# A Hymba block on one core: two quadrant sums of the gate weight made by accumulating transfers, and pair 2's spatial products placed later

## The reference, cut to what matters

```python
h = rms_norm(x, norm_mix_pre)                 # x: 2048 x 1024, float32
z = h @ w_in                                  # q, k, v, and the columns u and v of the gating unit
g_in = gelu(z[..., o3:])                      # 1024 columns: u (512), v (512)
vn = layer_norm(v, ln_g, ln_b)
s_out = u * (W_masked @ vn + b)               # 4 groups, blocks of 128 positions: the spatial products
```

## Time and profile before

| | us |
|---|---|
| median of 3 runs (1841.42 to 1842.73) | 1842.46 |
| the profiled execution | 1840.42 |
| its span, first to last instruction | 1838.6 |
| PE busy in it | 1818.6 (99%) |
| DVE busy | 1274.8 (69%) |
| ACT busy | 740.7 (40%) |
| POOL busy | 148.9 (8%) |

### The profile page before, as it was taken

One profiled execution on the slowest core, in us unless ns is written; L12 is line 12 of the kernel. 1 busy time (PEld: TensorE's weight loads), 2 busy tenths in 40 slices (PEclk: granted clock), 3 DMA queues, 4 the chain that ended last, 5 costly groups with the idle time before them and its releaser, 6 DMA issues.

```text
span 1838.6 us, 24806 instructions
## 1 busy us (share of the span) xinstructions
PE 1818.6 (99%) x9322; PEld 1527.1 (83%) x9322; DVE 1274.8 (69%) x1625; ACT 740.7 (40%) x1278; POOL 148.9 (8%) x162
## 2 busy tenths in 40 slices
PE   9999999999999999999999999999999999999998
PEld 7788899988888888888888888888887888888887
DVE  8879777864568777776767777676776755554564
ACT  7776566753345323233234322323223222332342
POOL 1111222210000000000000000000000000000244
PEclk9999999999999999999999999999999999999999
DMA  6886743345666333332344423432235664534655
GB/s 236 293 318 259 264 196 153 116 150 206 221 262 232 127 108 112 99 108 86 108 121 172 141 86 108 125 106 88 86 111 179 257 231 159 195 124 176 248 204 189
DMA packets 134324, 310.78 MB, mean 169 GB/s; under 512 B 6384, under 2 KB 85232, under 8 KB 121072
## 3 DMA queue, kind: packets, MB, share of 16 engines
q1 hardware_dynamic: 134256, 309.90, 48.1%
HBM read 207.64 MB, written 102.24 MB: 169 GB/s over the span
## 4 chain that ended last, share of the span: by engine, by line
PE 86%; DVE 2%; issue 0%; POOL 0%; ACT 0%; DVEq 0%; POOLq 0%
PE T L2028 7%; PE T L2029 7%; PE T L2030 7%; PE ZB L2365 4%; PE ZB L2367 4%; PE ZB L2366 4%; PE T L2367 4%; PE T L2365 4%; PE T L2366 4%; PE S L2367 3%; PE S L2365 3%; PE S L2366 3%; PE ZA L2367 3%; PE ZA L2365 3%; PE ZA L2366 3%; PE ZA L2028 2%
## 5 line engine op out<-in xcount | busy, mean ns | idle before, releaser
L2028 PE MATMUL T<-tb_hi,sb_hi 128*128 128x512 f32 x616 | 239.9, 390 | 1.3 <-DVE sb_lo L1914 1.2
L2030 PE MATMUL T<-tb_hi,sb_lo 128*128 128x512 f32 x616 | 239.7, 389 | 0.0
L2029 PE MATMUL T<-tb_lo,sb_hi 128*128 128x512 f32 x616 | 239.7, 389 | 0.0
L1201 ACT ACTIVATE sb_hi<-sb_raw 128x1408 fp32r<-128x1408 f32 x56 | 77.4, 1381 | 290.6 <-PE T L2030 275.8
L1777 DVE TENSOR_TENSOR t_lo<-t_raw,t_hi 128x1024 fp32r<-128x1024 f32 (+1 forms) x126 | 169.0, 1397 | 0.1
L2365 PE MATMUL ZB<-s_hi,t_hi 128*128 128x512 f32 x352 | 137.1, 389 | 1.1 <-DVE t_lo L1777 1.1
L2028 PEld LDWEIGHTS T<-tb_hi,sb_hi 128*128 128x128 f32 x616 | 115.6, 188 | 26.5 <-issue 1.9
L2365 PE MATMUL T<-s_hi,t_hi 128*128 128x512 f32 x352 | 137.0, 389 | 0.0
L2366 PE MATMUL ZB<-s_lo,t_hi 128*128 128x512 f32 x352 | 137.0, 389 | 0.0
L2366 PE MATMUL T<-s_lo,t_hi 128*128 128x512 f32 x352 | 136.9, 389 | 0.0
L2367 PE MATMUL ZB<-s_hi,t_lo 128*128 128x512 f32 x352 | 136.9, 389 | 0.0
(11 more groups left out here) (314 smaller groups left out, 4275.4 us busy)
## 6 DMA issues: line engine op xcount, KB each, us to landing
t_raw<-w_gu SPq DMA_DIRECT2D x42, 1024.0 KB, 4.7
act_d<-ac SPq DMA_DIRECT2D x22, 1792.0 KB, 8.0
sb_raw<-act_d SPq DMA_DIRECT2D x56, 704.0 KB, 4.1
h_d<-quarters SPq DMA_DIRECT2D x8, 1792.0 KB, 6.6
s_raw<-h_d SPq DMA_DIRECT2D x14, 1024.0 KB, 6.4
lb_hi<-hl_d SPq DMA_DIRECT2D x6, 1792.0 KB, 7.2
lb_lo<-hl_d SPq DMA_DIRECT2D x6, 1792.0 KB, 11.5
tb_raw<-w_dn SPq DMA_DIRECT2D x6, 1536.0 KB, 6.4
```

The lines of the kernel that those rows point to most:

```text
L1201: e.activation(sb_hi[it % 2][:, :, :], sb_raw[it % 2][:, :, :], ACT.Copy).then_inc(sb_hi_done, 1)
L2028: e.matmul(out_ap, lhi, rhi, start=start, stop=False)
L2029: e.matmul(out_ap, lhi, rlo, start=False, stop=False)
L2030: return e.matmul(out_ap, llo, rhi, start=False, stop=stop)
```

## The change

R3 and R4 are no longer subtracted on DVE. ACT writes a negated copy into the place of the sum (of B12 for R3, of R2 for R4), and a transfer issued by POOL then adds a quadrant from DRAM (B22, B21) onto it. POOL waits for all the constants before the first, and for the first to land before the second. The orders on ACT, DVE and PE are changed around it, and the numbers that waits on `w_sum` and `gel_done` count to are adjusted.

```diff
 # POOL, ahead of rstd_x(0)
+            def add_block(dst, src):
+                e.dma_start(dst[:, :, :], src, accum_op=ALU.add).then_inc(w_added, 16)
+            e.wait_ge(consts, 16 * 6)
+            e.wait_ge(b12_read, 2)
+            add_block(wu_raw[3], w_uv[B22, :, :, :])
+            e.wait_ge(w_sum, 3)
+            e.wait_ge(w_added, 16)
+            add_block(wu_raw[6], w_uv[B21, :, :, :])
             rstd_x(0)
-            e.wait_ge(consts, 16 * 6)
 # ACT
             wu_hi_part(6, wu_b12, slice(2, 4))
+            e.activation(wu_raw[3][:, :, :], wu_b12[:, :, :], ACT.Copy, scale=-1.0).then_inc(b12_read, 1)
...
+            e.wait_ge(in_done, 3)
+            e.activation(wu_raw[6][:, :, :], wu_raw[2][:, :, :], ACT.Copy, scale=-1.0).then_inc(w_sum, 1)
             stats_x(0)
-            e.wait_ge(w_sum, 3)
-            wu_hi_part(6, wu_raw[6])
             uv_copy(1, 0)
-            e.wait_ge(w_sum, 4)
+            e.wait_ge(w_added, 16)
             wu_hi_part(3, wu_raw[3])
             uv_copy(1, 1)
             gelu_v(0, 1)
             stats_x(1)
+            e.wait_ge(w_added, 32)
+            wu_hi_part(6, wu_raw[6])
+            scale_xq(2)
+            left_hi(2, 0)
             gelu_u(0, 0)
             gelu_v(0, 0)
             gelu_u(0, 1)
-            scale_xq(2)
-            left_hi(2, 0)
...
+            gelu_v(1, 0)
             gelu_u(1, 0)
-            gelu_v(1, 0)
             gelu_u(1, 1)
 # DVE: the two subtractions
-                if i == 3:
-                    e.tensor_tensor(wu_raw[3][:, :, :], wu_b22[:, :, :], wu_b12[:, :, :], ALU.subtract).then_inc(w_sum, 1)
-                if i == 6:
...
-                    e.tensor_tensor(wu_raw[6][:, :, :], wu_b21[:, :, :], wu_raw[2][:, :, :],
-                                    ALU.subtract).then_inc(w_sum, 1)
 # DVE: the order
-            wu_sum(6)
-            wu_sum(3)
+            e.wait_ge(w_sum, 3)
             wu_lo_part(2, wu_raw[2], 7)
             left_lo(1, 2)
-            wu_lo_part(3, wu_raw[3], 9)
+            wu_lo_part(3, wu_raw[3], 8)
             norm_stats(0, 1)
+            normed(0, 1)
             uv_u2(1)
-            wu_lo_part(6, wu_raw[6], 8)
+            wu_lo_part(6, wu_raw[6], 9)
             uv_u3(1)
-            normed(0, 1)
             left_sums(2)
...
             uv_upper(1)
             gate(0, 1)
-            gate(0, 0)
-            uv_lower(1)
             left_lo(2, 2)
             normed(1, 1)
+            uv_lower(1)
+            gate(0, 0)
             norm_stats(1, 0)
             normed(1, 0)
 # PE, behind product (j, i); spatial(j - 1, 1) comes first
-                    if i in (2, 4):
+                    if i in ((3, 4) if j == 2 else (2, 4)):
                         spatial(j - 1, 1 - i // 4)
```

More of the change, by code:

```diff
@@ L202, in build_kernel @@
     w_in_loaded, b11_rest = [sem(f"w_in_loaded{i}") for i in range(4)], sem("b11_rest")
-    b12_rest, b12_hi, b12_split = sem("b12_rest"), sem("b12_hi"), sem("b12_split")
+    b12_rest, b12_read, b12_split = sem("b12_rest"), sem("b12_read"), sem("b12_split")
     id_zero, pool_consts = sem("id_zero"), sem("pool_consts")
     xq_scaled, lsum_done, lhi_done, lsplit = sem("xq_scaled"), sem("lsum_done"), sem("lhi_done"), sem("lsplit")
-    w_sum, w_hi_done, w_split = sem("w_sum"), sem("w_hi_done"), sem("w_split")
+    w_sum, w_hi_done, w_split, w_added = sem("w_sum"), sem("w_hi_done"), sem("w_split"), sem("w_added")
     hl_out, norm_step = sem("hl_out"), sem("norm_step")
@@ L390, in load_wout @@
                 e.dma_start(wout_raw[c][:, :], w_out[chunk(c), :]).then_inc(wout_in[c], 16)
-            e.wait_ge(w_sum, 4 + 3)
+            e.wait_ge(w_sum, 3 + 3)
             e.dma_start(cs[:, :, :], rope).then_inc(cs_in, 16)
-            e.wait_ge(w_sum, 4 + 4)
+            e.wait_ge(w_sum, 3 + 4)
             e.wait_ge(w_split, 9 + 3)
@@ L793, in gelu_v @@
                     e.wait_ge(w_split, 2)
-                    e.wait_ge(w_sum, 4)
+                    e.wait_ge(w_sum, 2)
                     e.activation(dst[:, :], GU[0][1 + par], ACT.Gelu, scale=r).then_inc(gel_done, 1)
@@ L819, in wq_hi_part @@
                     src = {R1: wq_r1, R2: wq_r2}[t] if t in (R1, R2) else wq_raw[i]
-                    e.wait_ge(w_sum, 4 + {R1: 1, R2: 2, R3: 3, R4: 4}[t])
+                    e.wait_ge(w_sum, 3 + {R1: 1, R2: 2, R3: 3, R4: 4}[t])
                 e.activation(wq_hi[i][:, :, :], src[:, :, :], ACT.Copy).then_inc(w_hi_done, 1)
@@ L831, in _ @@
             e.wait_ge(w_in_loaded[B12], 16)
-            e.activation(wu_hi[6][:, 0:2, :], wu_b12[:, 0:2, :], ACT.Copy).then_inc(b12_hi, 1)
+            e.activation(wu_hi[6][:, 0:2, :], wu_b12[:, 0:2, :], ACT.Copy).then_inc(b12_read, 1)
             e.wait_ge(b12_rest, 16)
             wu_hi_part(6, wu_b12, slice(2, 4))
+            e.activation(wu_raw[3][:, :, :], wu_b12[:, :, :], ACT.Copy, scale=-1.0).then_inc(b12_read, 1)
             e.wait_ge(w_in_loaded[B22], 16)
@@ L1312, in gate @@
                 e.wait_ge(g_full, n + 1)
-                e.wait_ge(gel_done, 4 * j + (2, 4)[par])
+                e.wait_ge(gel_done, 4 * j + (3 if j == 1 else 2, 4)[par])
                 if j:
@@ L1323, in norm_stats @@
                 src = (bv12, bv22)[par]
-                e.wait_ge(gel_done, 4 * j + (3, 1)[par])
+                e.wait_ge(gel_done, 4 * j + (2 if j == 1 else 3, 1)[par])
                 e.bn_stats(st6[:, par, :], src[:, :]).then_inc(norm_step, 1)
@@ L1385, in wq_sum @@
                     e.wait_ge(w_split, 9 + 1)
-                    e.wait_ge(w_sum, 4 + 1)
+                    e.wait_ge(w_sum, 3 + 1)
                     e.tensor_tensor(wq_r2[:, :, :], wq_in[B22][:, :, :], wq_r1[:, :, :],
@@ L1395, in wq_sum @@
                     e.wait_ge(w_in_loaded[B21], 32)
-                    e.wait_ge(w_sum, 4 + 2)
+                    e.wait_ge(w_sum, 3 + 2)
                     e.tensor_tensor(wq_raw[6][:, :, :], wq_in[B21][:, :, :], wq_r2[:, :, :],
@@ L1410, in _ @@
             first_lo(1)
-            e.wait_ge(b12_hi, 1)
+            e.wait_ge(b12_read, 1)
             e.tensor_tensor(wu_lo[6][:, 0:2, :], wu_b12[:, 0:2, :], wu_hi[6][:, 0:2, :].bitcast(F32),
@@ L2082, in uv_product @@
                     if i == 0:
-                        e.wait_ge(gel_done, 4 * (j - 2) + 2)
+                        e.wait_ge(gel_done, 4 * (j - 2) + (3 if j == 3 else 2))
                     if i == 1 and j == 2:
```

3 lines of the change are left out of this document (removed).

## The result

The changed kernel took 1845.9 us (median of 20 runs, 1843.12 to 1847.88); the kernel before, in as many runs beside it, 1841.01 (1839.81 to 1842.73). The ratio is 1.0024, with a 95% interval from 1.0017 to 1.0031: slower by 4.9 us, where the forecast had 1.95. The median of before that the prediction started from (1842.46, 3 runs) was 1.45 high against the larger number of runs, so the absolute forecast of 1844.4 stands nearer to 1845.9 than its sum deserves. What follows goes by the differences. The profiled execution took 1845.38, 4.96 more than that of before.

A forecast was written before the change was run, and what follows sets the result against it. PE was taken as the bound (busy 99%), capping any gain at 3.5 us of waits; +1.35 at product (2, 0) and +0.6 at spatial (2, 1) took 1842.46 to 1844.4 us, range 1840.5 to 1848.5.

The forecast's parts named there:

- First negated copy free, `bp1`'s wait of 0.6 gone: ACT's first negated copy fills idle time at no cost; product (1, 4) loses its 0.6 us wait for `bp1`.
- R3 hidden: First adding transfer lands at about 33, R3 is wanted by about 38 for product (1, 3), so no wait.
- The adds, 6.5 and 8 us: POOL's two accumulating 1 MB transfers take 6.5 and 8 us, bounds 4.8 and 11.8 each.
- s = 42.2: Pair 1's second squares on ACT start at 42.2, bounds 40.6 and 43.8, after later-issued `xs` transfers; before, 41.12.
- The chain behind s: From pair 1's second squares through POOL and DVE: product (1, 6) at s+7.6, `left_sums(2)` at s+7.4.
- The limit for the second add: ACT's `wu_hi6` and `scale_xq(2)` stay slack if the second add lands by s+2.3 = 44.5.
- Product (2, 0) at 54.1: On PE, product (2, 0) starts at 54.1, 1.35 us later than 52.74, bounds -0.25 and +2.9.
- Pair 2: The removed 2.0 us norm wait at spatial (1, 1) is swallowed at spatial (2, 1), and 0.6 us is lost.
- The sum: Product (2, 0) +1.35 and spatial (2, 1) up to +0.6 give +1.95 us; bounds 1842.3 to 1846.8.
- Slow adds: Rival, 0.18: ACT's `wu_hi6` waits for a second add past 44.5; at 11.8 us each, 1849.8 us.
- POOL held by DVE: Rival, 0.07: the adds' descriptors are written only when DVE pauses, first at about 36; 1847.6 us.
- Gain: Rival, 0.20: `xs` lands in 5.2 us and the gated tiles' store does not bind; about -1.6, 1840.9 us.

The follow-up runs named there:

- no addition: Changed kernel with POOL's two transfers as plain loads of the same 1 MB, the sums left out: 1841.38 us, ratio 1.0005 to the kernel before.
- add early: Changed kernel with POOL's wait for the constants moved from ahead of the first adding transfer to later: 1843.98 us, ratio 1.0018 to the kernel before.
- xs early: Changed kernel with pair 1's two `xs` transfers loaded ahead of pair 2's left operand, into B12's place: 1841.24 us, ratio 1.0002 to the kernel before.
- both early: Changed kernel with pair 1's `xs` loaded early and the first adding transfer ahead of the wait for constants: 1840.1 us, ratio 0.9997 to the kernel before.
- The kernel with the scaling first: Kernel with early `xs` and early first add, plus ACT scaling pair 2's left operand before waiting for the second add: 1842.45 us, ratio 1.0009 to before.
- the filler: Changed kernel with 26 transposes of the identity on PE ahead of product (1, 6), inside its wait: 1845.61 us, ratio 1.0026 to the kernel before.
- pair 2's part alone: Kernel before with only pair 2's new order (spatial (1, 1) behind product (2, 3), reordered DVE and ACT): 1840.97 us, ratio 1.0001.
- The sums alone: Changed kernel with pair 2's reordering undone, keeping the accumulating transfers and pair 1's orders: 1845.37 us, ratio 1.0024 to the kernel before.

## Why the prediction was right or wrong

The profiles can be read together. Call s the start of pair 1's second squares and a the start of ACT's `wu_hi` for slot 6. The start of `left_sums(2)` is the later of s + 6.85 (the power, the norm, `bu2`, `wu_lo`, `bu3`) and a + 5.14 (`wu_hi`, then `scale_xq(2)`), and spatial (2, 1) follows some 37 us later.

| kernel | s | a | s + 6.85 | a + 5.14 | left_sums(2) | spatial (2, 1) |
|---|---|---|---|---|---|---|
| changed | 45.12 | 47.05 | 51.97 | 52.19 | 52.19 | 89.30 |
| no addition | 42.19 | 43.48 | 49.04 | 48.62 | 49.04 | 86.08 |
| add early | 44.70 | 45.99 | 51.55 | 51.13 | 51.55 | 88.59 |
| xs early | 39.50 | 44.15 | 46.35 | 49.29 | 49.29 | 86.21 |
| both early | 39.01 | 43.12 | 45.86 | 48.26 | 48.26 | 85.30 |
| before | | | | | 48.28 | 85.60 |

The two sums were fitted on rows of these kernels (no addition and both early); the other three check them, and agree within 0.01. The kernel with the scaling first has another order and isn't in the table.

**First negated copy free, `bp1`'s wait of 0.6 gone.** Right. `bp1` ran at 34.90 (forecast 34.55), and no wait for it is left. Most of the 0.35 was there before the change could act: in this execution PE began product (1, 0) at 31.54, in that of before at 31.16.

**R3 hidden.** Right, with less room: the add landed at 35.2, and `wu_hi(3)` started at 35.38 with no idle ahead of it. The forecast had 33, and 38 as the limit.

**The adds, 6.5 and 8 us.** This is the step that failed. They took 8.2 and 11.2. I took 6.5 as "near the quiet row, with one read more", and an add turned out to take twice the engine time of a copy. The bounds (4.8 and 11.8) held. The Trainium skill, "DMA: Bandwidth & Descriptors", section "Anatomy of one DMA — SWDGE (gpsimd) path", gives 2.0 us plus the bytes at 436 GB/s; the estimate from it, 4.4 us for 1 MB, is below the plain transfers (5.2 and 7.2, the second beside loads) and about half of the first add.

**s = 42.2.** Failed with it: 45.12, past the bound of 43.8. That bound counted an add as 2 MB, which is the right weight, but priced the further MB at the 1.6 us between two rows (6.8 less 5.2), where 1.05 MB take 2.5 at 420 GB/s. It also left the issue at 34.35 (it was 34.78) and took one time to landing for the pair: the second squares started 10.3 us after the first issue, with ACT waiting for them.

**The chain behind s.** Right, a little long: product (1, 6) at s + 7.1 (forecast 7.6) and `left_sums(2)` at s + 7.07 (7.4), since the power for the norm lasted 0.55 instead of 0.98. The limit for the second add was put at s + 2.3; by the table it is s + 1.71. The add was past it by 0.2, so in the changed kernel both branches end together, and no cure of one alone could have been read off it. Early `xs` works on both, which is why it recovers 4.3 us and the early add only 1.5.

**Product (2, 0) at 54.1.** It came at 58.17. Of the 4.07 that it was off, 2.9 are s, and the shorter chain takes some 0.4 back. The other 1.5 are the product at the low clock (`left_sums(2)` plus 4.46 gives 56.65), which I didn't foresee and which the filler shows to be worth nothing in the end.

**Pair 2.** That the 2.0 us are swallowed was right, in two kernels. The mechanism wasn't: I had the gates of pair 1 wait for the store, later than before, for a loss of 0.6. With pair 2's part alone the store (3.7 us) no longer binds, DVE's list behind ACT's scaling does, and spatial (2, 1) comes 0.36 earlier in the profile, with nothing to tell in the time. In the changed kernel the store took 3.8 us, and the gates start at 79.53 without a wait.

**The sum.** Its terms, +1.35 and +0.6, came out at spatial (2, 1) as 3.7 in all, none of it from pair 2, and at the median as 4.9. That is past the +4.3 at which the bounds of its terms end. That 1845.9 lies below 1846.8 all the same is luck: the median that it started from was 1.45 high.

**The rivals.** "Slow adds" had the right cause and the wrong place. I gave it 0.18, since it asked for 9.1 us each; the first stayed under that and the second made up for it. Its formula gives 1.95 + 2.55 = 4.5 us for a second add at 47.05, against a limit of 44.5, near the 4.9 measured, but that is luck: the limit moves with s, and against the limit of s + 1.71 the add was late by 0.2 only. What it left out is that a slow add holds up `xs`, and that this alone puts `left_sums(2)` at 51.97. "POOL held by DVE" is out: the first add was issued at 27.02 with DVE busy 1.00 from 27 to 28, and bytes moved from 28 on (74 GB/s in the mean from 28 to 30, 201 behind that). This agrees with the Trainium skill, "SBUF — State Buffer", section "Who interferes with whom", by which such subtractions have no mode that holds POOL's descriptors off. "Gain" is out by the time.

**What stays open.** Of the 4.96 us between the two profiled executions, 3.70 stand at spatial (2, 1). Of these, 0.38 were there at product (1, 0), ahead of all that is told here: PE's wait for the first rounded weights from ACT differs between executions (1.53 us at 10.07 in that of the changed kernel, 0.51 and 0.39 in those with the add early and without the addition), and the table's absolute times carry such a scatter. About 0.95 more come between 137.61 (spatial (4, 0), +3.69) and 174.04 (spatial (6, 1), 169.40 before, +4.64), and 0.3 behind that. In this stretch PE waits 0.28 for a low left part. That row in PE's timeline of the changed kernel:

```profile
144.43 0.50 PE L2104 MATMUL T<-wu_hi,lb_hi 128*128 128x512 f32 x1 [0.28 <-DVE lb_lo L1289]
```

A like wait is in the profiled executions with `xs` early (0.41) and with both early (0.28), which took 1.4 us more than the medians of their kernels, and not in those of before, of pair 2 alone, without the addition, or with the add early. The sums alone and the filler show no wait of 0.2 or more there, but the stretch is as long (36.1 and 36.2 us, against 35.5 before). So it looks like something that comes and goes between executions of the changed lists. I made no experiment on it, and how much of the median's 4.9 it is isn't shown; the differences at spatial (2, 1) (3.7 of 4.9, 3.0 of 3.35 with the add early, 0.5 of 0.7 without the addition) leave 0.2 to 1.2 us to it and to the start.

## What to carry to other kernels

Moving an addition from an engine into a transfer takes it off an engine's list, and here it put twice the bytes' time onto the transfer engines; price it there, and then price every plain transfer that travels beside it, which may be the one that is waited for. Before freeing an engine, ask whether PE waits for that engine's work or for its order: here DVE lost 4.6 us of subtractions and then stood idle for 6.6. When two branches end together (here 51.97 and 52.19), an edit that reaches only one can show little, so try an edit that works on both, or both edits at once.

## What the runs showed of the hardware

- An accumulating transfer of 1 MB (float32, DRAM onto SBUF, issued by POOL) kept the transfer engines at a share of 0.98 to 1.01 while 201 to 215 GB/s moved, against 401 to 434 for plain transfers at a share of 0.97 to 1.03. It took 8.2 us with one load behind it and 11.2 beside 1.5 MB of loads; plain ones in the same places took 5.2 and 7.2.
- POOL's instruction lasted 1.04 and 0.86 us for the accumulating transfers, 0.72 and 0.54 for the plain ones.
- During a wait of 4.2 us PE's granted clock fell to 0.50 (1.2 GHz), stayed there for about 5 us of the work behind it, and twelve matmuls took 5.16 us instead of 2.72; with a filler of 26 small matmuls and a wait of 1.72 us behind it, it stayed at 1.00.
